# Decoder layer on one core: the two bias tables on ScalarE's queue, the fill table behind the second rows of x, the bias product among three idle products

## The chip, the cores and the metric

One NeuronCore of a Trainium2 chip. The metric is device time in microseconds (us), the median of three runs. Engines are TensorE (PE in the profile; PEld is its weight load), VectorE (DVE), ScalarE (ACT), GpSimd (POOL) and SyncE (SP), whose queue issues most transfers.

## The reference

With these sizes (D = 1024, 256 tokens, DEPTH = 1) the reference is one layer and a final norm, in float32:

```python
y = rmsnorm(h, norm_mix[0])
y = moba_attention(y, a_w_in[0], a_w_out[0], rel_bias)   # one block of 256: causal softmax attention
h = h + y                                                # of 16 heads, with a T5 bias by distance
h = h + squared_relu_mlp(rmsnorm(h, norm_mlp[0]), mlp_up[0], mlp_down[0])
return rmsnorm(h, final_norm)
```

The bias of a head depends on the distance of the two tokens alone: `rel_bias[bucket(distance), head]`, and a masked pair (distance below 0) gets minus infinity.

## The kernel before

The tokens are two blocks of 128 rows (`tb` 0 and 1). The weights come from HBM in chunks of 1 MB into four slots `raw`; ScalarE rounds each half of a chunk to `w_hi` (fp32r), VectorE forms `w_lo = raw - w_hi`, and TensorE multiplies with both. The first chunk alone (the values of the first four heads, `v_first`) is multiplied in plain float32 straight from `raw`. Every engine has a program written out by hand, and semaphores order them; nothing schedules.

The start, which the change touches, runs so:

- SyncE's queue issues the two halves of row block 0 of x, two pieces of the V chunk, row block 1 of x (its landing is the semaphore `x_next`), two more pieces, then the first Q chunk.
- GpSimd builds the identity, then issues three small loads: `rel_sb` (32 x 16), `onehot_sb` (32 x 384, which distance falls in which bucket) and `fill_sb` (16 x 384, the mask). After these it forms the low halves of the turned rows of block 0 in two subtractions (line 249), and later stores and loads the bias vector.
- ScalarE issues `mix_rows` (8 x 128, the norm's gain), loads its function table, then takes part in the norm of block 0 (lines 650 to 593) and of block 1 (lines 660 to 586).
- TensorE runs 6 idle products of a tile of ones (`FILL`; line 475; each is two passes in the trace, so x12), turns `mix_rows` (line 482), turns the rows of block 0 (line 287, 8 transposes), starts `v_first(0)` (line 323), turns the rows of block 1 before k = 6 of it, ends `v_first(0)`, and then makes the bias product of the two tables (line 486). `v_first(1)` and the four units of the first Q and K chunks follow (lines 358 and 359). The first Q unit waits at its start for the low halves of the turned rows (`ylo_done`, `ylo0_pool`), and at k = 4 for `lo_done` 2, the second half of the Q chunk's low weights:

```python
                if first and k == 4:
                    pe.wait_ge(lo_done, 2)
```

- VectorE norms both blocks. For block 1 it waits for `x_next`, squares and sums half a row (line 957, reads `h_sb` twice), adds EPS (line 960), takes an inverse (line 811) and scales half of the rows (line 816). Lines 759, 831 are subtractions for low halves. It turns the bias product into the bias vector at line 972, behind `lo_tile(1, 1)`.

Of the kernel before, what the change touches and what calls it, by code (L numbers as in the profile page):

```python
# [36 lines left out]
HEADS = 16  # L37
# [12 lines left out]
WHOLE = 1  # L50
SPLIT0 = 2 * (MLP0 - WHOLE)
PIECES = 4
FILL = 6
YT_FIRST = 5
ROOT = 1.0 / 32
assert ROOT * ROOT * D == 1.0
# [4 lines left out]
BV = P + T  # L61
# [21 lines left out]
def build(nc, x, rel_bias, norm_mix, norm_mlp, mlp_up, mlp_down, w_in, w_out, final_norm,  # L83
# [9 lines left out]
    with ExitStack() as ctx:  # L93
        def sb(name, shape, dt=F32):
            return ctx.enter_context(nc.sbuf_tensor(name, shape, dt))

        def sem(name):
            return ctx.enter_context(nc.semaphore(name))
# [28 lines left out]
        onehot_sb = sb("onehot_sb", [BUCKETS, BV])  # L127
        fill_sb = sb("fill_sb", [HEADS, BV])
        bv_sb = sb("bv_sb", [HEADS, BV])
        rel_sb = sb("rel_sb", [BUCKETS, HEADS])  # L130
# [9 lines left out]
        bank = [ctx.enter_context(nc.psum_tensor(f"bank{i}", [P, 512], F32)) for i in range(8)]  # L140
# [4 lines left out]
        BIAS = 3  # L145
# [9 lines left out]
        x_next = sem("x_next")  # L155
        ident_made, tables_loaded = sem("ident_made"), sem("tables_loaded")
        mix_loaded, mix_turned, mix_ready = sem("mix_loaded"), sem("mix_turned"), sem("mix_ready")
        gain_next, bias_loaded = sem("gain_next"), sem("bias_loaded")
        bias_summed, bias_vec, bias_stored = sem("bias_summed"), sem("bias_vec"), sem("bias_stored")
# [78 lines left out]
        @block.gpsimd  # L238
        def _(pool):
            pool.wait_ge(warm_made, 1)  # L240
            nc.gpsimd.affine_select(ident[:], warm[:, 0:P], [[-1, P]], ALU.is_equal, 0.0, base=0,
                                    channel_multiplier=1).then_inc(ident_made, 1)
            nc.gpsimd.dma_start(rel_sb[:], rel_bias).then_inc(tables_loaded, 16)
            nc.gpsimd.dma_start(onehot_sb[:], bucket_onehot).then_inc(tables_loaded, 16)
            nc.gpsimd.dma_start(fill_sb[:], causal_fill).then_inc(fill_loaded, 16)
            for b in range(2):
                pool.wait_ge(yhi_done, b + 1)
                ks, tok = slice(4 * b, 4 * b + 4), slice(0, P)
                nc.gpsimd.tensor_tensor(yT[:, ks, LO, tok], yF[:, ks, tok], yT[:, ks, HI, tok].bitcast(F32),
                                        ALU.subtract).then_inc(ylo0_pool, 1)  # L250
            pool.wait_ge(bias_vec, 1)
            nc.gpsimd.dma_start(bias_dram, bv_sb[:]).then_inc(bias_stored, 16)
            pool.wait_ge(bias_stored, 16)

            def tiles(a):

                src = bass.AP(tensor=bias_dram.tensor, offset=bias_dram.offset + a * (4 * BV),
                              ap=[[1, P], [BV, 4], [1, T]])
                nc.gpsimd.dma_start(bias_sb[:], src).then_inc(bias_loaded, 16)

            tiles(0)
            nc.gpsimd.dma_start(gain[:], norm_mlp.partition_broadcast(P).rearrange("p a d -> p (a d)")
                                ).then_inc(gain_next, 16)

            for a in range(1, CHUNKS_IN):
                pool.wait_ge(biased, 4 * a)
                tiles(a)
            pool.wait_ge(y_done, 2 * TB)
            nc.gpsimd.dma_start(gain[:], final_norm.partition_broadcast(P)).then_inc(gain_next, 16)
# [3 lines left out]
        def _(pe):  # L273
            mm = nc.tensor.matmul
# [36 lines left out]
            def v_first(tb):  # L311

                acc = bank[UNIT[tb]][:, 0:CW]
                wf = cols(raw, 0)
                for k in range(KB):
                    if k == 6 and tb == 0:
                        transposes_first(1)
                    if k in ((0, 2, 4) if tb == 0 else (0, 4)):
                        pe.wait_ge(yf_done, k // 2 + 1 if tb == 0 else k // 4 + 4)
                    if tb == 0 and k % (KB // PIECES) == 0:  # L320
                        i = k // (KB // PIECES)
                        pe.wait_ge(v_piece[i] if i < PIECES - 1 else raw_full[0], 16)
                    last = mm(acc, yF[:, k, tb * P:(tb + 1) * P], wf[:, k, :], start=(k == 0), stop=(k == KB - 1))  # L323
                last.then_inc(unit_done, 1)
# [149 lines left out]
            def idle_product():  # L474
                mm(bank[IDLE][:, 0:256], warm[:, 0:P], warm[:], start=True, stop=True)

            pe.wait_ge(warm_made, 1)
            for _ in range(FILL):
                idle_product()
            pe.wait_ge(ident_made, 1)  # L480
            pe.wait_ge(mix_loaded, 16)
            nc.tensor.transpose(bank[MIX][:, 0:KB], mix_rows[:], ident[0:KB, 0:KB]).then_inc(mix_turned, 1)
            transposes_first(0)
            v_first(0)
            pe.wait_ge(tables_loaded, 32)
            mm(bank[BIAS][0:HEADS, 0:BV], rel_sb[:], onehot_sb[:], start=True, stop=True).then_inc(bias_summed, 1)
            v_first(1)

            for part in "qk":
# [61 lines left out]
        def _(act):  # L551
# [81 lines left out]
            def h_hi(f, par, i):  # L633
                act.wait_ge(s_done, 2 * f + i + 1)
                nc.scalar.copy(hT[:, par, i, HI, :], s_sb[:, i, :]).then_inc(hhi_done, 1)  # L635

            def step(f, par, first=False, last=False):
# [3 lines left out]
                for i in range(2):  # L641
# [2 lines left out]
                        hi_mlp(f + 2, par, 0, i, (up_done, 2 * f + 2))  # L644
                    h_hi(f + 1, 1 - par, i)

            nc.scalar.dma_start(mix_rows[:], norm_mix[0].rearrange("(k p) -> k p", p=P)).then_inc(mix_loaded, 16)
            nc.scalar.preload_act_table(ACT.Sqrt)
            act.wait_ge(x_half[0], 16)
# [434 lines left out]
```

## Time and profile before

| | |
|---|---|
| runs | 310.7, 310.87, 311.29 us; median 310.87 |
| profiled execution | 310.88 us, of which the span is 309.2 us |
| TensorE busy | 299.7 us, 97% of the span |
| VectorE, ScalarE, GpSimd busy | 205.8, 160.0, 9.3 us |
| the chain that ended last | PE 90%, DVE 4%, DMA 2%, ACT 1% |

A row of the timeline or of the chain gives the start in us from the span's start, the duration, the engine and line, and in brackets how long the engine stood idle and what released it. The chain of waits names what ended last; the timeline shows what stands around it. 0.2% of the time is 0.62 us.

### The profile page before, as it was taken

How to read it: one execution, taken by the hardware profiler on the slowest of the kernel's cores; microseconds unless marked ns; L12 is line 12 of the kernel's file. 1: busy time of each engine (PE TensorE's matmuls, PEld its weight loads, DVE VectorE, ACT ScalarE, POOL GpSimd, SP SyncE). 2: the span in 40 equal slices, each digit the busy share in tenths (PEclk: the TensorE clock that was granted, in tenths of full speed). 3: DMA queues.
4: the chain of work that ended last, by engine and by line, in shares of the span. 5: the costliest groups of instructions: out<-in, count | busy, mean ns of one | idle time of the engine just before them, and what ended most of it. 6: DMA issues, size and time to landing. Idle time of an engine off the chain costs nothing.

```text
span 309.2 us, 4658 instructions
## 1 busy us (share of the span) xinstructions
PE 299.7 (97%) x1679; PEld 254.0 (82%) x1679; DVE 205.8 (67%) x397; ACT 160.0 (52%) x293; POOL 9.3 (3%) x17
## 2 busy tenths in 40 slices
PE   7899999999999999999999999999999999999992
PEld 5588879888888888988888888888888888888881
DVE  3696995875884669686495476567558548557564
ACT  4685754854755435665354445447436445544422
POOL 2301000000000000000000000000000000000000
PEclk9999999999999999999999999999999999999999
DMA  6999988146166047366755746656565574620003
GB/s 221 354 282 357 355 282 270 73 137 272 68 187 223 2 142 229 119 174 221 224 185 144 259 148 184 215 164 221 158 199 208 144 238 161 166 105 0 0 3 136
DMA packets 36654, 55.87 MB, mean 181 GB/s; under 512 B 1128, under 2 KB 29840, under 8 KB 36640
## 3 DMA queue, kind: packets, MB, share of 16 engines
q1 hardware_dynamic: 35632, 52.43, 52.9%
q0 software_dynamic: 992, 3.25, 2.9%
q8 instruction: 9, 0.15, 0.2%
q14 instruction: 5, 0.04, 0.0%
q10 hardware_dynamic: 16, 0.00, 0.0%
HBM read 54.61 MB, written 1.07 MB: 180 GB/s over the span
## 4 chain that ended last, share of the span: by engine, by line
PE 90%; DVE 4%; DMA 2%; ACT 1%; issue 1%; SPq 1%; DVEq 0%; ACTq 0%
PE bank L403 36%; PE bank L358 26%; PE bank L359 13%; DMA h_sb<-in_x_dram 2%; PE bank L336 2%; PE bank L337 2%; PE bank L338 2%; PE bank L323 1%; PE bank L379 1%; PE bank L442 1%; PE bank L441 1%; PE bank L393 1%; PE bank L371 1%; DVE w_lo L759 1%; PE bank L369 1%
## 5 line engine op out<-in xcount | busy, mean ns | idle before, releaser
L759 DVE TENSOR_TENSOR w_lo<-raw,w_hi 128x1024 fp32r<-128x1024 f32 x94 | 112.7, 1220 | 58.2 <-ACT w_hi L559 56.2
L358 PE MATMUL bank<-yT,w_hi 128*128 128x512 f32 x368 | 131.6, 400 | 0.1
L559 ACT CAST w_hi<-raw 128x1024 fp32r<-128x1024 f32 x93 | 94.6, 1048 | 56.6 <-PE bank L403 56.6
L359 PE MATMUL bank<-yT,w_lo 128*128 128x256 f32 x368 | 103.2, 280 | 0.0
L358 PEld LDWEIGHTS bank<-yT,w_hi 128*128 128x128 f32 x368 | 69.1, 188 | 17.8 <-issue 1.3
L403 PE MATMUL bank<-w_hi,hT 128*128 128x512 f32 x256 | 71.8, 390 | 0.0
L359 PEld LDWEIGHTS bank<-yT,w_lo 128*128 128x128 f32 x368 | 69.5, 189 | 0.6
L403 PEld LDWEIGHTS bank<-w_hi,hT 128*128 128x128 f32 x256 | 47.0, 188 | 9.7
L403 PE MATMUL bank<-w_lo,hT 128*128 128x512 f32 x128 | 40.2, 390 | 0.0
L403 PEld LDWEIGHTS bank<-w_lo,hT 128*128 128x128 f32 x128 | 24.0, 188 | 5.2
L629 ACT COPY part<-bank 128x256 f32<-128x256 f32 x30 | 11.2, 373 | 23.3 <-PE bank L359 23.3
L403 PE MATMUL bank<-w_hi,oT 128*128 128x512 f32 x64 | 19.1, 398 | 0.0
L635 ACT CAST hT<-s_sb 128x256 fp32r<-128x256 f32 x32 | 13.1, 408 | 8.2 <-DVE s_sb L922 8.2
L616 ACT ACTIVATE probs<-probs,negmax 128x128 f32<-128x128 f32 (+1 forms) x32 | 14.2, 445 | 5.9 <-DVE negmax L855 5.7
L855 DVE CUSTOM_DVE_ANT_0 probs<-bank,bias_sb 128x128 f32<-128x128 f32 (+1 forms) x32 | 9.7, 350 | 9.5 <-PE bank L371 9.5
L917 DVE TENSOR_TENSOR z_sb<-bank,part 128x256 f32<-128x256 f32 x30 | 12.6, 421 | 4.6 <-ACT part L629 4.6
L927 DVE TENSOR_TENSOR hT<-s_sb,hT 128x256 fp32r<-128x256 f32 x32 | 13.4, 419 | 1.9 <-ACT hT L635 1.9
L922 DVE SCALAR_TENSOR_TENSOR s_sb<-z_sb 128x256 f32<-128x256 f32 x32 | 13.6, 426 | 1.1
L403 PEld LDWEIGHTS bank<-w_hi,oT 128*128 128x128 f32 x64 | 11.7, 188 | 2.7 <-issue 0.5
L336 PE MATMUL bank<-w_hi,yT 128*128 128x256 f32 x48 | 13.9, 289 | 0.0
L337 PE MATMUL bank<-w_lo,yT 128*128 128x256 f32 x48 | 13.6, 283 | 0.0
L338 PE MATMUL bank<-w_hi,yT 128*128 128x256 f32 x48 | 13.6, 282 | 0.0
(96 smaller groups left out, 247.2 us busy)
## 6 DMA issues: line engine op xcount, KB each, us to landing
raw<-in_mlp_up_dram SPq DMA_DIRECT2D x16, 1024.0 KB, 5.6
raw<-in_mlp_down_dram SPq DMA_DIRECT2D x16, 1024.0 KB, 4.9
raw<-in_a_w_in_dram SPq DMA_DIRECT2D x10, 1024.0 KB, 9.2
raw<-in_a_w_out_dram SPq DMA_DIRECT2D x4, 1024.0 KB, 4.9
bias_sb<-bias_by_distance POOLq DMA_DIRECT2D x4, 512.0 KB, 6.0
raw<-in_a_w_in_dram SPq DMA_DIRECT2D x4, 256.0 KB, 6.0
raw<-in_a_w_in_dram SPq DMA_DIRECT2D x2, 512.0 KB, 8.2
out_dram<-y_sb SPq DMA_DIRECT2D x4, 256.0 KB, 2.4
```

Source lines behind the costliest of these rows:

```text
L336: mm(acc, yT[:, k, HI, tok], wh[:, k, :], start=(k == 0), stop=False)
L337: mm(acc, yT[:, k, HI, tok], wl[:, k, :], start=False, stop=False)
L338: last = mm(acc, yT[:, k, LO, tok], wh[:, k, :], start=False, stop=(k == KB - 1))
L358: mm(dst[:], wh[:, k, own], yT[:, k, :, :], start=(k == 0), stop=False, skip_group_check=True)
L359: last = mm(dst[:, 0:T], wl[:, k, own], yT[:, k, HI, :], start=False, stop=(k == KB - 1), skip_group_check=True)
L403: last = mm(bank[ACC[tb][c]][:], lhs(l), w[:, r, c * 512:(c + 1) * 512], start=first, stop=(stop and l == LO))
L559: nc.scalar.copy(w_hi[:, slot, part_of], raw[:, slot, part_of]).then_inc(hi_done, 1)
L616: last = nc.scalar.activation(probs[:, s, own], probs[:, s, own], ACT.Exp, bias=negmax[:, s, tb:tb + 1], scale=-1.0, accum_out=rowsum[:, s ...
L635: nc.scalar.copy(hT[:, par, i, HI, :], s_sb[:, i, :]).then_inc(hhi_done, 1)
L759: v.tensor_tensor(w_lo[:, slot, own], raw[:, slot, own], f32(w_hi[:, slot, own]), ALU.subtract).then_inc(lo_done, 1)
L922: v.scalar_tensor_tensor(s_sb[:, i, :], z_sb[:, i, :], 0.0, z_sb[:, i, :], ALU.max, ALU.mult).then_inc(s_done, 1)
L927: v.tensor_tensor(hT[:, par, i, LO, :], s_sb[:, i, :], f32(hT[:, par, i, HI, :]), ALU.subtract).then_inc(hT_ready, 1)
```

## The change

The two tables go to ScalarE's queue, ahead of `mix_rows`; GpSimd loads the fill table only once row block 1 of x has landed; three idle products instead of six; and the bias product moves from behind `v_first(0)` to behind the idle products.

```diff
-FILL = 6
+FILL = 3
@@ gpsimd
-            nc.gpsimd.dma_start(rel_sb[:], rel_bias).then_inc(tables_loaded, 16)
-            nc.gpsimd.dma_start(onehot_sb[:], bucket_onehot).then_inc(tables_loaded, 16)
+            pool.wait_ge(x_next, 16)
             nc.gpsimd.dma_start(fill_sb[:], causal_fill).then_inc(fill_loaded, 16)
@@ tensor
             for _ in range(FILL):
                 idle_product()
+            pe.wait_ge(tables_loaded, 32)
+            mm(bank[BIAS][0:HEADS, 0:BV], rel_sb[:], onehot_sb[:], start=True, stop=True).then_inc(bias_summed, 1)
             pe.wait_ge(ident_made, 1)
             pe.wait_ge(mix_loaded, 16)
             nc.tensor.transpose(bank[MIX][:, 0:KB], mix_rows[:], ident[0:KB, 0:KB]).then_inc(mix_turned, 1)
             transposes_first(0)
             v_first(0)
-            pe.wait_ge(tables_loaded, 32)
-            mm(bank[BIAS][0:HEADS, 0:BV], rel_sb[:], onehot_sb[:], start=True, stop=True).then_inc(bias_summed, 1)
             v_first(1)
@@ scalar
+            nc.scalar.dma_start(onehot_sb[:], bucket_onehot).then_inc(tables_loaded, 16)
+            nc.scalar.dma_start(rel_sb[:], rel_bias).then_inc(tables_loaded, 16)
             nc.scalar.dma_start(mix_rows[:], norm_mix[0].rearrange("(k p) -> k p", p=P)).then_inc(mix_loaded, 16)
```

TensorE's order from its first product to the first Q unit, before (a row is a line of the kernel, the operation, what it writes and reads, and how many in a row):

```order
L475 MATMUL bank<-warm 128x256 x6
L482 MATMUL bank<-ident,mix_rows 128x8
L287 MATMUL bank<-ident,y_sb 128x128 x8
L323 MATMUL bank<-raw,yF 128x256 x6
L287 MATMUL bank<-ident,y_sb 128x128 x8
L323 MATMUL bank<-raw,yF 128x256 x2
L486 MATMUL bank<-onehot_sb,rel_sb 16x384
L323 MATMUL bank<-raw,yF 128x256 x8
L358 MATMUL bank<-yT,w_hi 128x512
```

And TensorE's order now, over the same stretch:

```order
L474 MATMUL bank<-warm 128x256 x3
L480 MATMUL bank<-onehot_sb,rel_sb 16x384
L483 MATMUL bank<-ident,mix_rows 128x8
L286 MATMUL bank<-ident,y_sb 128x128 x8
L322 MATMUL bank<-raw,yF 128x256 x6
L286 MATMUL bank<-ident,y_sb 128x128 x8
L322 MATMUL bank<-raw,yF 128x256 x10
L357 MATMUL bank<-yT,w_hi 128x512
```

The bias product left the place between the two halves of `v_first` (2 and 8 products are now 10 in a row) and stands between the idle products and the turn of `mix_rows`.

GpSimd's order from the identity to the store of the bias vector, before:

```order
L241 AFFINE_SELECT ident<-warm 128x128 [waits warm_made]
L243 DMA rel_sb<-in_rel_bias_dram 32x16
L244 DMA onehot_sb<-in_bucket_onehot_dram 32x384
L245 DMA fill_sb<-in_causal_fill_dram 16x384
L249 TENSOR_TENSOR yT<-yF,yT 128x4x128 [waits yhi_done] x2
L252 DMA bias_by_distance<-bv_sb 16x384 [waits bias_vec]
```

And GpSimd's order now:

```order
L241 AFFINE_SELECT ident<-warm 128x128 [waits warm_made]
L244 DMA fill_sb<-in_causal_fill_dram 16x384 [waits x_next]
L248 TENSOR_TENSOR yT<-yF,yT 128x4x128 [waits yhi_done] x2
L251 DMA bias_by_distance<-bv_sb 16x384 [waits bias_vec]
L258 DMA bias_sb<-bias_by_distance 128x4x256 [waits bias_stored]
```

Two loads are gone from GpSimd, and the third, with a new wait for `x_next`, stands directly ahead of the two subtractions.

## Rows read from the trace of the kernel before

**Rows 1.** The page: busy time by engine, and the granted clock in 40 slices.

```profile
PE 299.7 (97%) x1679; PEld 254.0 (82%) x1679; DVE 205.8 (67%) x397; ACT 160.0 (52%) x293; POOL 9.3 (3%) x17
...
PEclk9999999999999999999999999999999999999999
```

**Rows 2.** The chain of waits in the first 40 us: start, us, what.

```profile
2.73 6.36 DMA h_sb<-in_x_dram
9.11 1.18 DVE y_sb L957
10.32 0.17 DVE stat L960
...
11.10 0.50 DVE y_sb L816
...
13.60 0.74 PE bank L486 x2
14.34 3.65 PE bank L323 x16
```

**Rows 3.** Timeline of TensorE, 0 to 18 us.

```profile
1.27 4.36 PE L475 MATMUL bank<-warm 128*128 128x256 f32 x12 [1.27 <-DVE warm L939]
5.56 0.22 PE L482 MATMUL bank<-ident,mix_rows 8*128 8x8 f32 x1
6.46 1.06 PE L287 MATMUL bank<-ident,y_sb 128*128 128x128 f32 x8 [0.67 <-DVE y_sb L816]
...
9.95 1.10 PE L323 MATMUL bank<-raw,yF 128*128 128x256 f32 x4 [0.50 <-DMA raw<-in_a_w_in_dram]
```

**Rows 4.** Timelines of all engines, 8 to 20 us.

```profile
8.46 1.27 POOL L249 TENSOR_TENSOR yT<-yF,yT 128x512 fp32r<-128x512 f32 x1 [5.24 <-ACT yT L593]
...
13.06 0.62 ACT L593 CAST yT<-yF 128x512 fp32r<-128x512 f32 x1 [0.73 <-DVE yF L825]
...
17.81 1.23 DVE L759 TENSOR_TENSOR w_lo<-raw,w_hi 128x1024 fp32r<-128x1024 f32 x1 [0.72 <-ACT w_hi L559]
...
19.11 0.19 PEld L358 LDWEIGHTS bank<-yT,w_hi 128*128 128x128 f32 x1
```

**Rows 5.** Lines 831 and 816: duration min/median/max in ns, first and last start, forms.

```profile
L831 DVE TENSOR_TENSOR yT<-yF,yT x2: 684/684/685, 15.8 to 16.4; 128x512 fp32r<-128x512 f32 x2
L816 DVE TENSOR_SCALAR y_sb<-h_sb,stat x3: 347/353/486, 6.0 to 11.1; 128x256 f32<-128x256 f32 x2, 128x512 f32<-128x512 f32 x1
```

**Rows 6.** Timeline of ScalarE, 0 to 5 us (ACTq: its queue issues).

```profile
0.81 0.59 ACTq L647 DMA_DIRECT2D mix_rows<-in_norm_mix_dram  x1
1.45 1.28 ACT L648 ACT_TABLE_LOAD   x1 [1.45 <-PEq L1075]
3.50 0.63 ACT L650 ACTIVATE squares<-h_sb 128x512 f32<-128x512 f32 x1 [0.78 <-DMA h_sb<-in_x_dram]
...
4.62 0.42 ACT L653 ACTIVATE squares<-h_sb 128x256 f32<-128x256 f32 x1 [0.40 <-DMA h_sb<-in_x_dram]
```

**Rows 7.** DMA issues, 0 to 40 us: KB each, median us to landing; and one issue's duration.

```profile
h_sb<-in_x_dram SPq DMA_DIRECT2D x2, 256.0 KB, 3.0
...
onehot_sb<-in_bucket_onehot_dram POOLq DMA_DIRECT2D x1, 48.0 KB, 4.3
...
2.73 0.50 POOL L245 DMA_DIRECT2D fill_sb<-in_causal_fill_dram  x1
```

**Rows 8.** Line 475: durations in 1 to 3.4 us, then in 4.6 to 5.7 us.

```profile
L475 PEld LDWEIGHTS bank<-warm x6: 289/337/337, 1.3 to 3.1; 128*128 128x128 f32 x6
...
L475 PEld LDWEIGHTS bank<-warm x3: 190/190/190, 4.6 to 5.0; 128*128 128x128 f32 x3
```

**Rows 9.** Windows of 0.5 us: busy by engine, granted clock, DMA share, GB/s last.

```profile
3.50:4.00 0.50, 0.50 (x3) 0.34 (x2) 0.00 (x0) 0.49 (x1) 0.00 (x0) 1.00 0.57 120
4.00:4.50 0.50, 0.50 (x3) 0.44 (x2) 0.00 (x0) 0.23 (x2) 0.00 (x0) 1.00 0.71 145
...
6.50:7.00 0.50, 0.50 (x5) 0.50 (x6) 0.17 (x3) 0.18 (x1) 0.00 (x0) 1.00 0.95 373
```

## The prediction

> **What bounds the kernel now.** I read the page first: TensorE is busy 97% of the span [rows 1], so after the start nearly every gain must be an earlier start of TensorE's dense stream. The chain of waits over the first 40 us came next [rows 2]: it runs through the landing of row block 1 of x at 9.09 us, VectorE's sum of squares (line 957), the small steps of the norm, its scaling (line 816), the transposes, the end of `v_first(0)`, 0.74 us of bias product, and 3.65 us of 16 passes of `v_first(1)`. Third, the timelines, since the chain names only what came last. On TensorE [rows 3] they show 0.50 us of idle time ahead of 9.95, for a V piece; it then waits again until VectorE has scaled the rows of block 1, 11.10 + 0.50 = 11.60 [rows 2]. Around 18 us [rows 4] they show what stands next to the chain: line 759, the low half of the Q chunk, ends at 17.81 + 1.23 = 19.04, and the weight load of k = 4, which waits for exactly that, starts at 19.11. It is the fifth weight of a steady stream, so TensorE did not visibly stop there, but it had some 0.07 us to spare and no more.
>
> **The change part by part.**
>
> *The bias product leaves its place between the halves of `v_first`.* Its two passes cost 0.74 us on the chain [rows 2], so `v_first(1)` can start at 13.60 and end 0.74 us sooner. What it reads is there: the first rows of block 1 are turned before ScalarE's cast of them at 13.06 [rows 4]. Then the first Q unit meets two waits. The low halves of line 831 end at 16.4 + 0.685 = about 17.1 [rows 5], ahead of the new end of `v_first(1)`, 14.34 + 3.65 - 0.74 = 17.25 [rows 2], and cost next to nothing. But k = 4 waits for the 19.04 of line 759 as before. ScalarE and VectorE ahead of line 759 hang on the turned rows of block 1 (13.06 [rows 4]), not on the bias product, so they don't move with it. Of the 0.74 us some 0.04 us (19.11 to 19.07) reach k = 4, and nothing behind it can gain more. Ends: 0 and 0.07 us. I take 0.04 us gained; the other 0.70 us turn into a wait at k = 4.
>
> *The bias product in its new place.* ScalarE issues onehot at 0.81 and rel 0.59 us later [rows 6]. The trace has no such load on this queue; the bounds for landing are 3.0 us (SyncE's 256 KB) and 4.3 us (the same table on GpSimd's queue) [rows 7], so both tables are there between 4.4 and 5.7 us. Six passes instead of twelve leave TensorE free at about 4.0: 12 took 4.36 us from 1.27, the first ones at the slower pace. The product itself costs 0.74 us at full clock, about 1.3 us at half (below). It ends between 5.1 and 7.0, I take 5.6. The transposes of block 0 start at 6.46 [rows 3], and even 0.5 us late they would be covered by the 0.50 us that TensorE waits ahead of 9.95. Cost nothing; without that cover up to 0.5 us.
>
> *Two more issues ahead of ScalarE's work.* 2 x 0.59 = 1.18 us [rows 6]. `mix_rows` is issued at 2.0 instead of 0.81. It had landed by 5.56 [rows 3], so within 4.75 us; now at 6.75 at the latest, at 5.5 by the faster bound. The table load starts at 1.45 + 1.18 = 2.63 and ends at 3.91, so the first square starts 0.41 us later than 3.50; with its 0.63 and the read of its sum it ends near 4.7 and pushes the second square from 4.62 by 0.1 us. The norm of block 0 is 0.1 us late, and the same 0.50 us cover it. Cost nothing.
>
> *The fill table behind `x_next`.* 24 KB fewer ahead of row block 1, at the 373 GB/s of a full stretch [rows 9] 0.06 us. The table is wanted by line 972, behind line 759 at 19.0 [rows 4]; issued at 9.1 and landing some 4.3 us on like onehot [rows 7], it is there by 13.5. What is queued behind the new wait on GpSimd is line 249. It ran at 8.46 to 9.73 [rows 4]. Now GpSimd waits until 9.1, issues for 0.50 us [rows 7], and starts line 249 near 9.65. Nobody needs it before 17 us by its result, but VectorE does meet it. Line 957 reads 512 elements twice and took 1.18 us [rows 2], while line 831, also 512 elements and two inputs, takes 0.684 us [rows 5]. The excess is 0.49 us, and it fits line 249: from 9.73 on, 0.56 us were left. I read this as VectorE held until GpSimd ended. With line 249 moved, line 957 should take 0.69 us and end near 9.80, 0.49 us sooner. But then line 249 starts at 9.80 and holds until 9.80 + 1.27 = 11.07. In that stretch fall lines 960 and 811 (one element, one input) and line 816, which would now be due at 10.61. Line 816 needs 0.486 us for 512 elements and 0.353 for 256 [rows 5], so 256 more elements cost 0.133 us, 0.52 ns each; it moves faster than line 831 (0.684 for the same 512), seemingly two elements at a time, and may need both paths. If it is held, it starts at 11.07 instead of 11.10: nothing gained. If it is not, the whole 0.49 us are gained. Nothing in this trace shows such an instruction beside line 249; I take "held", as it is nearest in traffic to line 957, which was. The Trainium skill, "SBUF — State Buffer", section "Who interferes with whom", says that VectorE and GpSimd share one port pair as an exclusive lock, taken by two-input instructions against GpSimd's reads and by `tensor_scalar` in its two-port mode. The excess of line 957 agrees with it. By that rule the term is 0.03 us; by the row of line 957 alone, with line 816 free, it would be 0.49 us.
>
> Sum against the profiled execution (310.88 us, within 0.01 of the median 310.87): 0.04 + 0.03 from VectorE's 11.07, and the 0.06 of x, of which I count none as landing is not that regular. 310.88 - 0.07 = 310.8.
>
> **The rivals.**
>
> *A. VectorE's line 957 is freed and line 816 is not held: 310.35 us.* 310.88 - 0.49 - 0.04. For it: the excess is real, and ScalarE's half of the rows starts sooner in any case. Against it: line 249 lands right on line 816.
>
> *B. Slower: GpSimd's displaced subtraction holds line 960.* Line 960 stood at 10.32 [rows 2]; if a one-element step is held too, it starts at 11.07 instead, 0.75 us late, and with it everything down to line 759. TensorE's spare of 0.07 us is all there is against it: 310.88 + 0.7 = 311.6. It decides as soon as line 249 starts between 9.05 and 10.3, which it does. For it: one `tensor_scalar` like line 816. Against it: one element can't be split over two paths. A milder form is that GpSimd's issue waits for line 957: line 249 then runs from 9.80 + 0.50 to 11.57, and line 816 is 0.47 us late: 311.3.
>
> *C. The clock.* The granted clock reads 1.00 throughout [rows 1], but weight loads of the same line take 337 ns until about 4.3 us and 190 ns after [rows 8], so the array goes from 1.2 to 2.4 GHz there, after TensorE has been busy since 1.27. With three products and a product of 16 columns behind a gap it may stay at 1.2. Then the transposes and the first passes take up to twice their time; the 12 passes of `v_first` ahead of the transposes of block 1, 0.23 us each [rows 2], would start near 8.2 at 0.42. If full clock comes after as long a busy stretch as before, 6.46 + 3.1 = 9.6, they end by 11.6, in time for the 11.60 of line 816: 0. If it comes only when they are nearly done, 0.9 us: 311.7. The Trainium skill, "TensorE: Matmul & The Clock Gate", section "What's actually happening", also ties full clock to sustained activity; it gives no other price here.
>
> *D. Row block 1 lands at another time.* The transfers run at 120 and 145 GB/s in 3.5 to 4.5 us against 373 later [rows 9], after GpSimd's tables were issued. If these are the cause, up to 0.5 x (253 + 228) / 373 = 0.64 us come back on the chain: 310.2. If the 50 KB on ScalarE's queue push the rows of x instead, I estimate 0.2 us: twice the 0.13 us that 50 KB take at 373 GB/s, less the 0.06 of the fill table: 311.1.
>
> **How the numbers follow.** My forecast, all hidden but 0.07 us, 0.52, with a range of its own of 310.6 to 311.1; A 0.15; B 0.11 in both forms; C 0.09, of which half costs nothing measurable; D 0.13, 0.09 of it faster. The predicted time is 310.8. The range 310.2 to 311.5 reaches to A and to D's gain, and into B. Less than 0.2% either way, 0.62 us, is about what a measurement of this kernel can't tell from no change: faster than 310.25 needs D at its full price or A with part of D, 0.15; slower than 311.5 needs B in full or C's late form, 0.13; the rest, 0.72.
>
> **What would show it.** Line 486 gone from between the passes of line 323, and a wait for VectorE's `w_lo` ahead of the fifth weight load of the first Q unit, which still starts near 19.1. Line 957 at about 0.69 us, GpSimd's subtraction at 9.7 to 11.1, and line 816 starting at its end. Wrong if line 816 starts near 10.6 (A), line 960 near 11.1 (B), weight loads after 6.5 us take 337 ns (C), or line 957 starts away from 9.1 (D).

## The result and the profile after

The changed kernel takes 312.01 us (median of 8 runs, 311.69 to 312.42) against 310.91 us for the kernel before on the same chip (8 runs, 309.81 to 311.29). The ratio is 1.0039, 95% interval 1.0028 to 1.0051: slower, by 1.1 us, outside the predicted range. The profiled execution took 311.97 us with a span of 310.3 us, 1.1 us more than before.

Most lines moved by one in the new file: 474 is the idle product, 480 the bias product, 286 the transposes, 322 `v_first`, 826 the turned rows, 958 the sum of squares of block 1, 817 its scaling, 248 GpSimd's subtraction, 760 the low half of a weight. The timeline of the changed kernel, 0 to 20 us:

```profile
0.81 0.43 ACTq L646 DMA_DIRECT2D onehot_sb<-in_bucket_onehot_dram  x1
1.27 2.93 PE L474 MATMUL bank<-warm 128*128 128x256 f32 x6 [1.27 <-DVE warm L940]
4.01 0.63 ACT L651 ACTIVATE squares<-h_sb 128x512 f32<-128x512 f32 x1 [0.38 <-DMA h_sb<-in_x_dram]
4.45 1.46 PE L480 MATMUL bank<-onehot_sb,rel_sb 32*16 32x384 f32 x2 [0.25 <-DMA rel_sb<-in_rel_bias_dram]
...
6.58 1.94 PE L286 MATMUL bank<-ident,y_sb 128*128 128x128 f32 x8 [0.48 <-DVE y_sb L817]
...
8.56 0.69 DVE L826 TENSOR_TENSOR yF<-bank,mixT 128x512 f32<-128x512 f32 x1 [0.43 <-PE bank L286]
8.69 0.63 ACT L661 ACTIVATE squares<-h_sb 128x512 f32<-128x512 f32 x1
8.72 0.68 POOL L244 DMA_DIRECT2D fill_sb<-in_causal_fill_dram  x1 [7.14 <-DMA h_sb<-in_x_dram]
9.17 2.09 DVE L958 CUSTOM_DVE_ANT_0 y_sb<-h_sb 128x512 f32<-128x512 f32 x1
...
9.42 1.27 POOL L248 TENSOR_TENSOR yT<-yF,yT 128x512 fp32r<-128x512 f32 x1
...
12.07 0.49 DVE L817 TENSOR_SCALAR y_sb<-h_sb,stat 128x512 f32<-128x512 f32 x1
...
12.62 1.10 PE L286 MATMUL bank<-ident,y_sb 128*128 128x128 f32 x8 [0.55 <-DVE y_sb L817]
```

Read it against [rows 3] and [rows 4]. The first transposes begin 0.12 us later than before, as expected, but take 1.94 us instead of 1.06. So VectorE's last turned block (line 826) ends only at 9.25. Row block 1 of x took 5.7 us from its issue at 2.72 to its landing, against 6.4 before: it is there at 8.4, 0.7 us sooner than in the profile before, and finds VectorE busy. GpSimd, released by the same landing at 8.72, issues the fill table and then begins its subtraction at 9.42. Line 958 is nominally begun at 9.17 and ends at 11.26, 0.57 us after the subtraction's end at 10.69: it took 2.09 us instead of the 1.18 of [rows 2]. TensorE's own slow passes did not end last here: it stood idle 0.55 us until line 817 was done. Line 817 stands 0.97 us later than line 816 did.

The half clock is seen in the weight loads; the granted clock of the windows reads 1.00 in both kernels, so it does not tell this. Line 286 of the changed kernel between 0 and 9 us (duration min/median/max in ns, first and last start), and `v_first`'s line 322:

```profile
L286 PEld LDWEIGHTS bank<-ident,y_sb x8: 182/231/231, 6.5 to 7.9; 128*128 128x128 f32 x8
```

```profile
L322 PEld LDWEIGHTS bank<-raw,yF x32: 190/190/338, 8.1 to 17.4; 128*128 128x128 f32 x32
```

A load of 337 ns goes with 1.2 GHz and one of 190 ns with 2.4 GHz, as in [rows 8]; for the transposes it is 231 against 140 ns. Full clock came during `v_first(0)`, near 10 us, instead of near 4.3.

At the other end of the start, VectorE's low half of the Q chunk and TensorE's load for k = 4:

```profile
L760 DVE TENSOR_TENSOR w_lo<-raw,w_hi x1: 1225/1225/1225, 18.8 to 18.8; 128x1024 fp32r<-128x1024 f32 x1
```

```profile
19.29 0.19 PEld L358 LDWEIGHTS bank<-yT,w_lo 128*128 128x128 f32 x1
20.06 0.19 PEld L357 LDWEIGHTS bank<-yT,w_hi 128*128 128x128 f32 x1 [0.59 <-DVE w_lo L760]
```

The weight load of k = 4 now stands idle 0.59 us for this weight (the products themselves 0.27 us); before it did not. The first Q unit now waits at its start too, for the low halves of the turned rows of block 1 (line 832, done at 18.07):

```profile
16.78 1.29 DVE L832 TENSOR_TENSOR yT<-yF,yT 128x512 fp32r<-128x512 f32 x2
18.14 0.19 PEld L357 LDWEIGHTS bank<-yT,w_hi 128*128 128x128 f32 x1 [0.51 <-issue]
```

That wait is hidden behind the one at k = 4, which ends later. The low half that k = 4 waits for began at 17.81 us [rows 4] and begins at 18.8 now. In both kernels the span is that time plus 291.4 to 291.5 us. So the place where the change acts on the end is this one event, and the experiments are read by it.

### The profile page after: what moved, and what is told of

It is laid out like the page before. It is cut to its first block, busy times and chain, and to the rows that moved or that the text cites. A ratio compares the mean times of both kernels' runs of the same rounds, so it can differ in the third digit from the quotient of the medians.

```text
span 310.3 us, 4646 instructions
## 1 busy us (share of the span) xinstructions
PE 300.6 (97%) x1673; PEld 254.3 (82%) x1673; DVE 206.8 (67%) x397; ACT 159.8 (52%) x293; POOL 8.4 (3%) x15
## 4 chain that ended last, share of the span: by engine, by line
PE 85%; DMA 6%; DVE 4%; ACT 3%; issue 1%; DVEq 0%; ACTq 0%
PE bank L402 35%; PE bank L357 24%; PE bank L358 12%; DMA bias_sb<-bias_by_distance 3%; PE bank L335 2%; PE bank L336 2%; PE bank L337 2%; DMA bias_by_distance<-bv_sb 2%; PE bank L378 1%; PE bank L441 1%; PE bank L440 1%; PE bank L392 1%; DMA h_sb<-in_x_dram 1%; PE bank L286 1%; PE bank L370 1%
```

## The experiments

Every ratio is to the kernel before, measured on the same chip in the same rounds; runs that were made together share that measurement. Each has 4 or 5 rounds, 8 to 12 runs. An edit that adds or takes out lines moves the line numbers by one or two: 957, 958, 959 and 960 are all VectorE's sum of squares of block 1, and 816 to 819 the scaling.

**Six idle products in the changed kernel.**

```diff
-FILL = 3
+FILL = 6
```

> The changed kernel with six idle products again, all else as changed. Theory 'clock first' (full clock comes late, so VectorE is late at its sum of squares of block 1 and GpSimd's subtraction goes first): weight loads of the transposes of block 0 take some 0.14 us again, line 958 starts at the landing of x near 8.7 and takes 0.69 us, and the time falls by about 1 us to some 311.0 or below. Theory 'order alone' (GpSimd's wait and issue put its subtraction onto line 958 at any clock): line 958 still takes 1.4 to 2.1 us and the time stays within 0.3 us of 312.0. It also shows the product's own cost at the start: if transposes of block 0 begin more than 0.5 us after 6.46, the product in its new place is late.

Measured: 311.01 us against 310.53, ratio 1.0020 (1.0005 to 1.0036). Its timeline:

```profile
7.28 1.09 PE L286 MATMUL bank<-ident,y_sb 128*128 128x128 f32 x8
...
8.47 0.68 POOL L244 DMA_DIRECT2D fill_sb<-in_causal_fill_dram  x1 [6.89 <-DMA h_sb<-in_x_dram]
...
9.09 0.68 DVE L958 CUSTOM_DVE_ANT_0 y_sb<-h_sb 128x512 f32<-128x512 f32 x1
...
9.32 1.58 POOL L248 TENSOR_TENSOR yT<-yF,yT 128x512 fp32r<-128x512 f32 x1 [0.17 <-ACT yT L592]
...
10.59 0.59 DVE L817 TENSOR_SCALAR y_sb<-h_sb,stat 128x512 f32<-128x512 f32 x1
```

The transposes run at full clock, VectorE comes first, and its sum takes 0.68 us; GpSimd's subtraction is the one that is lengthened, to 1.58. 'Order alone' falls. By the ratio half of the loss is back, not all; the two intervals overlap a little. Why not all is not shown. The bias product behind six idle products made the transposes begin at 7.28 instead of 6.46, and VectorE began its sum only at 9.09, some 0.9 us behind the landing (5.4 us after the issue at 2.72), where 'at the landing' had been expected: line 826 ran until 9.17. But this profile is of a run of 310.49 us, faster than the profile of the kernel before, so it can't show what the median lost.

**Three idle products in the kernel before**, the same line the other way.

> The kernel before with three idle products instead of six, nothing else. 'Clock first': TensorE is idle from about 4.2 until 5.6, full clock comes only near 10, the transposes of block 0 take 1.9 us, VectorE's line 957 starts late or meets the subtraction for longer, and the time rises by 0.3 to 1.0 us to 311.2 to 311.9. 'Order alone': the time stays at 310.9 within 0.2.

Measured: 311.09 against 310.53, 1.0018 (1.0007 to 1.0029). The idle products alone, with nothing else of the change, slow the kernel. Its trace, of the slowest of its 11 runs (311.7 us), shows both costs:

```profile
6.12 1.94 PE L287 MATMUL bank<-ident,y_sb 128*128 128x128 f32 x8 [1.73 <-DVE y_sb L816]
...
7.85 4.83 PE L323 MATMUL bank<-raw,yF 128*128 128x256 f32 x12
...
8.41 1.26 POOL L249 TENSOR_TENSOR yT<-yF,yT 128x512 fp32r<-128x512 f32 x1 [5.19 <-ACT yT L593]
8.71 1.51 DVE L957 CUSTOM_DVE_ANT_0 y_sb<-h_sb 128x512 f32<-128x512 f32 x1
```

The twelve passes of `v_first` end at 12.68, so the transposes of block 1 start at 12.52 though line 816 is done at 11.53. Here TensorE's own slow passes end last, by 1.0 us, and not the longer sum of squares.

**The fill table last, and the fill table early**, both in the changed kernel with three idle products.

```diff
-            pool.wait_ge(x_next, 16)
-            nc.gpsimd.dma_start(fill_sb[:], causal_fill).then_inc(fill_loaded, 16)
@@ behind the two subtractions
+            nc.gpsimd.dma_start(fill_sb[:], causal_fill).then_inc(fill_loaded, 16)
```

> The changed kernel, with the fill table issued behind GpSimd's two subtractions and no wait for x. Three idle products stay. 'Clock first': the transposes of block 0 still take 1.9 us and end near 8.5; GpSimd's first subtraction starts when its input is cast, near 8.8, and still beats line 958, which ends near 10.6 instead of 11.2: the time is about 311.4. 'Order alone': nothing but the wait and the issue was the trouble, the time is back at 310.9 or below. If the fill table, issued near 14.7, comes late for the bias vector, line 973 waits and the time is above 312.

```diff
-            pool.wait_ge(x_next, 16)
```

> The changed kernel without the wait for x: the fill table is issued at once, as before. Three idle products stay. 'Clock first': as with the fill table last, GpSimd's subtraction starts near 8.8 and line 958 ends near 10.6, the time is about 311.4, half of the loss is back. 'Order alone': all of it is back, 310.9 or below. If the transfers ahead of x are what moved its landing from 9.09 to 8.65, the landing shows whether the fill table counts in that.

Measured: 1.0029 (1.0019 to 1.0039; 311.43 us) and 1.0028 (1.0006 to 1.0051; 311.50 us). The line without a wait:

```profile
9.24 1.26 POOL L247 TENSOR_TENSOR yT<-yF,yT 128x512 fp32r<-128x512 f32 x1 [7.03 <-ACT yT L591]
9.54 1.51 DVE L957 CUSTOM_DVE_ANT_0 y_sb<-h_sb 128x512 f32<-128x512 f32 x1
```

GpSimd still goes first and VectorE's sum takes 1.51 us instead of 2.09. In the changed kernel the subtraction's input was cast by 8.78 (8.16 + 0.62), and it began 0.64 us later because of the issue; that is the 0.58 us. The times lie where 'clock first' put them, but the intervals overlap with that of the changed kernel: by the ratios the wait and issue cost some 0.1%, not clear of the noise, and this part is shown in the traces only. Row block 1 of x landed 5.8 us after its issue in both profiles, against 5.7 in the changed kernel, so the fill table does not count in that.

**GpSimd's subtraction late, in the kernel before.**

```diff
             for b in range(2):
+                pool.wait_ge(rows0_dve, 3)
                 pool.wait_ge(yhi_done, b + 1)
```

> The kernel before, GpSimd's first subtraction made to wait until VectorE has scaled its half of block 1 (rows0_dve 3); tables, products and idle products as before. 'The pair is held' (a GpSimd subtraction under way holds VectorE's two-input sum): line 957 takes 0.69 us instead of 1.18, the second half of the Q chunk's low weights starts 0.5 us sooner after the landing of x, and the time is 0.3 to 0.5 us (0.1 to 0.16%) below before, less if TensorE is then what ends last. 'Not held': no change within 0.1%, or slower, since the subtraction's second half comes later than 13.7; both must be done by 17.

Measured: 309.74 us (309.54 to 310.20) against 310.60, ratio 0.9973 (0.9962 to 0.9983). It beats the kernel before, and by its ratio the changed one.

```profile
8.38 0.69 DVE L958 CUSTOM_DVE_ANT_0 y_sb<-h_sb 128x512 f32<-128x512 f32 x1 [0.17 <-DMA h_sb<-in_x_dram]
...
9.88 0.49 DVE L817 TENSOR_SCALAR y_sb<-h_sb,stat 128x512 f32<-128x512 f32 x1
...
10.46 2.50 POOL L250 TENSOR_TENSOR yT<-yF,yT 128x512 fp32r<-128x512 f32 x2 [7.24 <-DVE y_sb L817]
```

The second low half begins at 16.59 us, and the span is 307.9. In this profile the event comes 1.22 us sooner than in that of before, and the two parts can be told apart: the sum of squares started 0.73 us sooner (8.38 against 9.11), because x had landed sooner, and from its start to the event it is 8.21 us instead of 8.70, which is the 0.49 us of the hold. The measured gain, 0.86 us, is more than the hold; what the rest is, is not shown.

**The subtraction directly behind the sum of squares, in the kernel before** (`pool.wait_ge(square0_dve, 2)` in the same place).

> The kernel before, GpSimd's first subtraction made to wait for VectorE's sum of squares of block 1 (square0_dve 2), so that it runs beside lines 960, 811 and 816 and beside nothing else. The prediction's step 'line 816 is held': line 957 takes 0.69 us, lines 960 and 811 keep their 0.15 us, and line 816 starts or ends only at the subtraction's end, about 0.5 us later than it could: the time equals before within 0.1%. Rival A of the prediction, 'line 816 is free': it takes 0.49 us at once, and the time is 0.1 to 0.16% below before.

Measured: 310.14 against 310.60, 0.9987 (0.9974 to 0.9999).

```profile
8.54 0.69 DVE L958 CUSTOM_DVE_ANT_0 y_sb<-h_sb 128x512 f32<-128x512 f32 x1 [0.37 <-DMA h_sb<-in_x_dram]
...
9.28 0.15 DVE L961 TENSOR_SCALAR stat<-stat 128x1 f32<-128x1 f32 x1
9.33 1.27 POOL L250 TENSOR_TENSOR yT<-yF,yT 128x512 fp32r<-128x512 f32 x1 [6.11 <-DVE stat L958]
...
9.85 0.16 DVE L812 RECIPROCAL stat<-stat 128x1 f32<-128x1 f32 x1 [0.42 <-ACT stat L581]
...
10.05 0.83 DVE L817 TENSOR_SCALAR y_sb<-h_sb,stat 128x512 f32<-128x512 f32 x1
```

The scaling takes 0.83 us instead of 0.49 and ends 0.28 us behind the subtraction's end at 10.60. So it is held, but loses 0.34 us only, as it was due just 0.55 us before that end; the one-element steps keep their 0.15 and 0.16 us. The ratio alone would not decide: 0.13% below before is what was expected of rival A. The 0.83 us in the trace decide: there the gain against before is the sum's 0.49 us less the scaling's 0.34.

**The same late subtraction in the changed kernel**, three idle products:

> The changed kernel (three idle products, fill table behind x), with both of GpSimd's subtractions behind line 817 (rows0_dve 3). Full clock still comes late. 'Collision': line 958 takes 0.69 us, and 1.0 to 1.4 us come back as far as TensorE lets them: it is still at half clock for the first passes of v_first, so the transposes of block 1 start near 11.2 to 12.7; the time is 311.0 to 311.5 against the changed kernel's 312.0. 'Clock alone': TensorE's own late passes set the time, it stays near 312.

Measured: 311.07 against 310.60, 1.0017 (0.9997 to 1.0037). Line 959 takes 0.68 us at 9.13; line 818 is done at 11.12, but the transposes of block 1 start at 11.46, behind passes that began at half clock (the last is modelled to end at 11.62). By the ratios some 0.2% is back; the interval still meets that of the changed kernel.

**More idle products behind the bias product**, in the changed kernel:

```diff
             mm(bank[BIAS][0:HEADS, 0:BV], rel_sb[:], onehot_sb[:], start=True, stop=True).then_inc(bias_summed, 1)
+            for _ in range(3):
+                idle_product()
```

> The changed kernel with three more idle products behind the bias product (three ahead, three behind), all else as changed. 'Clock first': TensorE is busy from 1.3 us to about 6.5 with one gap of 0.3 to 0.7 us for the tables, the transposes of block 0 run at full clock (weight loads 0.14 us), line 958 starts at the landing of x and takes 0.69 us, and the time is back at that of before, or up to 0.3 us above where the idle products end after 6.5. 'Clock needs an unbroken stretch' or 'order alone': the transposes still take 1.9 us or line 958 still 2 us, and the time stays near 312.

Measured: 312.31 against 310.60, 1.0035 (1.0009 to 1.0060). 'Clock first' had this wrong; the median and the profile are as the second case of the expectation has them. But five of its 12 runs lie at 310.1 to 310.8 us and seven at 312.2 to 313.8, so the median stands for the slower group only (by the two medians alone the ratio would be 1.0055). The profile is of that group:

```profile
4.37 1.46 PE L480 MATMUL bank<-onehot_sb,rel_sb 32*16 32x384 f32 x2 [0.17 <-DMA rel_sb<-in_rel_bias_dram]
...
5.76 2.93 PE L474 MATMUL bank<-warm 128*128 128x256 f32 x6
...
8.82 1.94 PE L286 MATMUL bank<-ident,y_sb 128*128 128x128 f32 x8
```

TensorE was busy from 1.27 to 8.7 us but for 0.17 us, and still ran the idle passes and the transposes at 1.2 GHz. In this profile the added products only delayed the transposes. Six idle products in a row brought full clock by 7.0 us in each of the seven traces that have them; the same six with the bias product in their middle did not here. Whether they did in the five faster runs no trace shows.

**Both undone in the changed kernel**: six idle products and the late subtraction.

> The changed kernel with six idle products and GpSimd's subtractions behind line 818 (rows0_dve 3): both suspected costs undone, tables on ScalarE's queue, product behind the idle products and fill table behind x stay. If the two costs are all of the loss, the time is that of the kernel before with the subtraction late, ratio 0.997 to 0.998. If the product in its new place costs too (with six idle products it ended near 7.2 and the transposes of block 0 began 0.8 us late), the ratio is 0.999 to 1.001.

Measured: 310.18 against 310.24, 0.9994 (0.9981 to 1.0006). That is the second case of the expectation: the time is back at that of before, but 0.2% remains to the kernel before with the late subtraction (0.9973), which is the like to compare with, as the late subtraction also frees VectorE of a hold that the kernel before had. The transposes of block 0 start at 7.44 here. In this profile x landed at 9.7, 7.0 us after its issue, so they ended in time all the same: from the start of the sum at 9.75 to the event it is 8.22 us, as in the kernel before with the late subtraction, and the trace does not show a cost.

**The tables on ScalarE's queue alone**, in the kernel before:

```diff
-            nc.gpsimd.dma_start(rel_sb[:], rel_bias).then_inc(tables_loaded, 16)
-            nc.gpsimd.dma_start(onehot_sb[:], bucket_onehot).then_inc(tables_loaded, 16)
@@ scalar
+            nc.scalar.dma_start(onehot_sb[:], bucket_onehot).then_inc(tables_loaded, 16)
+            nc.scalar.dma_start(rel_sb[:], rel_bias).then_inc(tables_loaded, 16)
             nc.scalar.dma_start(mix_rows[:], norm_mix[0].rearrange("(k p) -> k p", p=P)).then_inc(mix_loaded, 16)
```

> The kernel before with the two tables on ScalarE's queue ahead of mix_rows, alone: six idle products, the bias product in its old place, the fill table early on GpSimd's queue. 'The queue is harmless': ratio 0.9985 to 1.0015; ScalarE's first square starts 0.4 us later, at about 4, and the transposes of block 0 start at 6.3 to 6.6. Rival D of the prediction: x lands at another time by the queue alone, gain of up to 0.6 us (0.998) or loss of 0.2 us (1.0007) with the landing in the trace to match.

Measured: 310.31 against 310.24, 1.0003 (0.9989 to 1.0017). The queue is harmless in the time, within some 0.2%. Its profile is not as expected:

```profile
4.46 0.63 ACT L650 ACTIVATE squares<-h_sb 128x512 f32<-128x512 f32 x1 [0.83 <-DMA h_sb<-in_x_dram]
...
7.03 1.06 PE L285 MATMUL bank<-ident,y_sb 128*128 128x128 f32 x8
```

The first square waits for the first half of row block 0 and starts at 4.46, not near 4, and the transposes of block 0 at 7.03, not by 6.6. This holds in all profiles: with the tables on GpSimd's queue (five of them) the first square starts at 3.45 to 3.62, and with the tables on ScalarE's (nine) at 3.90 to 4.46, each time upon that landing. So the 50 KB ahead do push the first rows of x, by 0.3 to 1.0 us; with six idle products the time does not show it.

**Three idle products and the late subtraction in the kernel before.**

> The kernel before with three idle products and GpSimd's subtractions behind line 817 (rows0_dve 3): the late clock without the collision. 'The clock costs only through the collision': ratio 0.997 to 0.998, as with six idle products. 'The clock costs by TensorE's own passes too': the twelve half-clock passes of v_first end at 11 to 12.7, the transposes of block 1 wait for them, and the ratio is 0.999 to 1.001.

Measured: 311.06 against 310.24, 1.0026 (1.0011 to 1.0041). Without any collision the late clock costs by itself; against the 0.9973 with six idle products, some 0.5%, the largest single effect found. The transposes of block 1 begin at 11.34 in its profile, 0.4 us after line 817 is done at 10.93, and VectorE's sum starts at 8.94, half a us after the landing of x at 8.4, 5.7 us from its issue.

**The bias product back in its old place**, in the kernel with both undone:

```diff
-            pe.wait_ge(tables_loaded, 32)
-            mm(bank[BIAS][0:HEADS, 0:BV], rel_sb[:], onehot_sb[:], start=True, stop=True).then_inc(bias_summed, 1)
@@ between v_first(0) and v_first(1)
+            pe.wait_ge(tables_loaded, 32)
+            mm(bank[BIAS][0:HEADS, 0:BV], rel_sb[:], onehot_sb[:], start=True, stop=True).then_inc(bias_summed, 1)
```

> As the run before with six idle products and GpSimd's subtractions late in the changed kernel, but with the bias product back in its old place between v_first(0) and v_first(1); the tables stay on ScalarE's queue and the fill table behind x. That run measured a ratio of 0.9994, and the kernel before with the subtraction late 0.9973. If the product's place behind six idle products costs the 0.2% between them, by the late start of block 0's transposes, the ratio is 0.997 to 0.998 and those transposes start near 6.5 instead of 7.44. If the tables' queue or the fill table's wait costs it, the ratio stays at 0.999 to 1.000.

Measured: 310.10 against 310.40, 0.9987 (0.9971 to 1.0004). The transposes start at 6.44 as expected, but the ratio lies between the two cases and its interval takes in both. Whether the product's place behind six idle products costs 0.1 to 0.2% stays open.

**Idle products and subtraction, taken together.** Ratios to the kernel before; each is good to 0.1 to 0.2%:

| kernel | subtraction as it was | subtraction late |
|---|---|---|
| before, six idle | 1 | 0.9973 |
| before, three idle | 1.0018 | 1.0026 |
| changed, three idle | 1.0039 | 1.0017 |
| changed, six idle | 1.0020 | 0.9994 |

Three idle products instead of six cost 0.2% in three of the four pairs and 0.5% in the fourth. The late subtraction gains 0.2 to 0.3% in three of four, the kernel before among them, and nothing where only the idle products of the kernel before were cut: there TensorE's own passes end last. Kernels that are alike in both and differ in the rest of the change lie 0.2% apart in three of four pairs, the changed one slower; in the fourth (three idle, late) they are equal within the noise.

**One event for all.** The start of the second low half of the Q chunk, and the span less that:

| profile | x, issue to landing | sum of squares of block 1 took | low half starts | span | difference |
|---|---|---|---|---|---|
| before | 6.4 | 1.18 | 17.81 | 309.2 | 291.4 |
| changed | 5.7 | 2.09 | 18.8 | 310.3 | 291.5 |
| changed, six idle | 5.4 | 0.68 | 17.41 | 308.8 | 291.4 |
| changed, fill early | 5.8 | 1.51 | 18.58 | 309.9 | 291.3 |
| before, three idle | 5.4 | 1.51 | 18.64 | 310.0 | 291.4 |
| before, subtraction late | 5.6 | 0.69 | 16.59 | 307.9 | 291.3 |
| before, subtraction behind the sum | 5.8 | 0.69 | 17.10 | 309.0 | 291.9 |
| changed, both undone | 7.0 | 0.69 | 17.97 | 309.3 | 291.3 |

In the six profiles that are not in the table the difference is 291.3 to 291.5. The 291.9 is the one exception: there TensorE waits 0.5 us more for VectorE's `qT`, later on. A single profile moves with the landing of x (8.1 to 9.7 us in these traces), so ratios decide and traces explain.

## Why the prediction was wrong

- *The bias product leaves its place.* Right in its end: what TensorE gained there became waits, and k = 4 still ended last, for the very weight that was named. But the wait is in two parts. The low halves ahead of the first Q unit, which were to cost next to nothing, hold its first weight load for 0.51 us, and that of k = 4 then for 0.59.
- *The bias product in its new place.* The tables landed at 3.8 and 4.4 us, at the early bound or before; the product ran at half clock and took 1.46 us, where 1.3 was given. It ended at 5.9, and the transposes began at 6.58. It was as late as was allowed for, and with three idle products its place cost little by itself.
- *Two more issues on ScalarE.* The first square began at 4.01 (3.91 was worked out), but not for the reason given: the table load was over at 3.63, and the square waited for the first half of row block 0, which landed later than before in every kernel with the tables on this queue. The queue alone is not seen in the time, 1.0003.
- *GpSimd and line 816 "held".* Right as a mechanism: 0.83 us instead of 0.49, one-element steps untouched (with six idle products in the changed kernel line 961 took 0.15 us in the middle of GpSimd's subtraction), so rivals A and B in its first form are out. The term of 0.03 us was too small even so: a held scaling ended 0.28 us behind the subtraction, not a full 0.49, so by that row line 816 would have ended at 11.35, 0.25 us sooner than before. But the whole step presumed that VectorE's sum would be first at the pair, since both wait for the landing of x. With TensorE at half clock VectorE was still busy with line 826 at that moment, and GpSimd had the pair first.
- *Rival C, the clock: the step that failed.* It had 0.09, half of it "costs nothing measurable", because I counted only TensorE's own twelve passes against the 11.60 of line 816. But in the profile of every kernel with three idle products the transposes of block 0 ran at half clock. Left out was what waits on the slow transposes: line 826 on VectorE, 0.9 us later, and with it the sum of squares, which lost its slack and its precedence and ended at 11.26 where 9.80 was forecast. Measured alone (three idle products in the kernel before) it costs 0.18%; without the collision on either side, 1.0026 against 0.9973, about 0.5%.
- *The milder form of B.* GpSimd's issue did put the subtraction 0.6 us later and onto the sum. Priced 0.47 us for line 816; it struck line 958 instead, for 0.58 us in the traces, and was worth some 0.1% of the time, not clear of the noise.
- *Rival D.* Row block 1 of x landed at 8.4 instead of 9.1, but it did so in other profiles with nothing changed in the queues (8.1 to 8.5 in four of them). The tables' queue has no measurable effect on the time, so GpSimd's small tables are not shown to slow the transfers. Its slower form came true for another transfer: the first half of row block 0 is what ScalarE's tables push back.

So the step that failed is that the late clock was to cost nothing beyond TensorE's own passes. Undoing both, the idle products and the collision, brings 1.0039 to 0.9994, which is clear of the noise; each alone brings about half, 1.0020 and 1.0017, and these intervals still meet that of the changed kernel. In the changed kernel as it stands, 0.18% is what the idle products cost alone, and the other 0.2% goes away with the late subtraction (1.0017, against 1.0026 for the kernel before with the same two edits). That this is all does not follow: with six idle products and the late subtraction the changed kernel is still 0.2% behind its like. That part, of the product's place, the tables' queue or the fill table, stays open.

The Trainium skill, "SBUF — State Buffer", section "Who interferes with whom", says that whoever of VectorE and GpSimd issues first has the shared pair for the whole instruction. The traces agree in both orders: VectorE's sum took 0.68 us and GpSimd's subtraction 1.58 when VectorE was first, 1.51 and 1.26 when GpSimd was. The changed kernel's own profile fits only if GpSimd counts as first, though VectorE's row begins 0.25 us sooner (the last point of this document).

## What to carry to other kernels

Idle products buy a state of the clock, and here three of them with a small product behind did not replace six in any of four traces, nor did six split up by the small one in the one trace of that kind: read the weight loads' durations of the first real work, not the granted clock alone. When work at the start is slowed, follow who waits for it on every engine, since what is lost there may be the order in which two engines reach a shared resource. A helper's instruction that shares such a resource with the critical engine should wait until the critical one has passed; one wait was worth 0.27% here, against the 0.39% that the whole change cost and the 0.02% that it was forecast to gain.

## What the hardware showed that I had not expected

- Full clock came at very different moments under the same unbroken series of six idle products from 1.27 us on: near 4.3 us in the profile before and with the late subtraction, near 5.4 in two others, between 5.7 and 6.5 in two, and just before 7.0 in one. With three it came between about 9 and 12 in six profiles. The moments are read from the first weight load that takes the shorter time, so they are as fine as the loads are dense.
- The granted clock of the windows reads 1.00 while weight loads take 337 ns instead of 190.
- A stretch that was busy from 1.27 to 8.7 us but for 0.17 us, with a product of 32 rows and 16 columns in it, still ran at 1.2 GHz at its end, and the runs of that kernel fell into two groups, 310.1 to 310.8 and 312.2 to 313.8 us.
- Two small tables, 50 KB together, issued on another queue at the same time as the first half of x, made that half land 0.3 to 1.0 us later: in nine profiles against five, with no overlap between them.
- A sum of squares that VectorE had nominally begun 0.25 us ahead of GpSimd's subtraction was held through the whole of it (9.17 against 9.42, end at 11.26). GpSimd was issuing its DMA at 9.17; whether the issue held the pair already was not separated.
